# The MLP of a two-block transformer step as two Strassen passes with the hidden layer in DRAM

## The reference

```
h2 = rms_norm(x, norm2_g)
u = jnp.square(jax.nn.relu(jnp.einsum('bsd,df->bsf', h2, w_up)))      # 1024 x 1024 times 1024 x 4096
x = x + jnp.einsum('bsf,fd->bsd', u, w_down)                          # 1024 x 4096 times 4096 x 1024
```

## Time and profile before

| | |
|---|---|
| median of 3 runs | 2311.85 us (2310.8 to 2312.58) |
| the profiled execution's own time | 2313.34 us |
| its span, first to last instruction | 2311.6 us |
| PE busy | 2233.6 us, 97% |
| DVE, POOL, ACT busy | 1319.2, 941.1 and 802.0 us |
| the MLP block | from 1643.4 us to the end |

### The profile page before, as it was taken

The page is one execution under the profiler, slowest core; times in us unless marked ns, Lnnn a source line. Parts: engine busy times, 40 slices in busy tenths (PEclk is TensorE's granted clock), DMA queues, the critical chain, the costliest instruction groups (busy, mean ns, idle before and its releaser), DMA issues. The chain is left out here.

```text
span 2311.6 us, 30049 instructions
## 1 busy us (share of the span) xinstructions
PE 2233.6 (97%) x10722; PEld 1854.4 (80%) x10722; DVE 1319.2 (57%) x2544; ACT 802.0 (35%) x1491; POOL 941.1 (41%) x732
## 2 busy tenths in 40 slices
PE   7999989999999999999999999999999999999997
PEld 7778777778877888888888788888888888888886
DVE  6666674516444666666666582334365565556467
ACT  5444424200004555555554131212333323323322
POOL 3232445535542322313313364553356355554534
PEclk9999999999999999999999999999999999999999
DMA  6220114212324323323322472222110110110211
GB/s 216 94 75 19 42 55 162 83 65 89 111 97 132 107 79 92 100 66 104 87 82 83 164 254 92 92 100 92 55 55 28 64 63 18 64 64 22 68 46 73
DMA packets 177605, 199.79 MB, mean 86 GB/s; under 512 B 56360, under 2 KB 126536, under 8 KB 177520
## 3 DMA queue, kind: packets, MB, share of 16 engines
q1 hardware_dynamic: 100352, 122.47, 16.1%
q10 hardware_dynamic: 77168, 76.19, 10.6%
HBM read 156.63 MB, written 50.40 MB: 90 GB/s over the span
## 5 line engine op out<-in xcount | busy, mean ns | idle before, releaser
L157 POOL TENSOR_TENSOR w_hi<-w_raw,zero 128x512 fp32r<-128x512 f32 x224 | 271.3, 1241 | 967.3 <-PE ps L202 847.5
L202 PE MATMUL ps<-a_hi,w_hi 128*128 128x512 f32 x1664 | 606.7, 405 | 7.4 <-PEq L1654 3.3
L202 PE MATMUL ps<-a_hi,w_lo 128*128 128x512 f32 x1664 | 586.8, 393 | 0.0
L202 PE MATMUL ps<-a_lo,w_hi 128*128 128x512 f32 x1664 | 584.7, 392 | 0.0
L202 PEld LDWEIGHTS ps<-a_hi,w_lo 128*128 128x128 f32 x1664 | 313.8, 189 | 69.3
L202 PEld LDWEIGHTS ps<-a_hi,w_hi 128*128 128x128 f32 x1664 | 314.8, 189 | 62.5 <-issue 9.2
L202 PEld LDWEIGHTS ps<-a_lo,w_hi 128*128 128x128 f32 x1664 | 315.2, 189 | 53.4
L2342 DVE TENSOR_TENSOR res<-res,ps 128x512 f32<-128x512 f32 x384 | 244.7, 682 | 118.0 <-PE ps L202 108.6
L162 POOL TENSOR_TENSOR w_lo<-w_raw,w_hi 128x512 fp32r<-128x512 f32 x224 | 299.7, 1370 | 4.4
L202 PE MATMUL ps<-w_hi,a_hi 128*128 128x512 f32 (+1 forms) x640 | 245.7, 384 | 7.5 <-PEq L1123 2.2
L202 PE MATMUL ps<-w_hi,a_lo 128*128 128x512 f32 (+1 forms) x640 | 244.1, 381 | 0.0
(11 more groups left out here) (206 smaller groups left out, 3301.9 us busy)
## 6 DMA issues: line engine op xcount, KB each, us to landing
w_raw<-in_w_in_dram SPq DMA_DIRECT2D x32, 1024.0 KB, 5.2
feat_fm<-stage ACTq DMA_DIRECT2D x68, 256.0 KB, 2.1
mlp_raw_x<-in_w_up_dram SPq DMA_DIRECT2D x28, 512.0 KB, 4.1
conv_in<-feat_fm ACTq DMA_DIRECT2D x24, 512.0 KB, 5.8
qkv_tm<-stage_tm ACTq DMA_DIRECT2D x5, 2048.0 KB, 6.9
res<-in_x_dram SPq DMA_DIRECT2D x16, 512.0 KB, 6.4
w_raw<-in_w_out_dram SPq DMA_DIRECT2D x8, 1024.0 KB, 5.0
qk_raw<-qkv_tm ACTq DMA_DIRECT2D x32, 256.0 KB, 3.9
```

Of the source, the lines that this page charges most:

```text
L157: hi = nc.gpsimd.tensor_tensor(w_hi[slot][:, k:k + 2, :], w_raw[:, k:k + 2, :], zero[:, 0:1].unsqueeze(2).to_broadcast([P, 2, CW]), ALU.add)
L202: last = nc.tensor.matmul(out_of(o), lhs, rhs(o), start=first and n == 0, stop=final and n == 2)
```

## The change

The MLP becomes two passes with the hidden layer u in DRAM between them. The norm n3 gets a function of its own (`phase_norm_last`) and also prepares operand sums for the first pass.

1. **Up pass, Strassen** over tokens, model features and hidden features: eight groups of 512 hidden features, seven products of 24 matmuls each (`up_tile`). ACT copies the first product of each quarter of u from PSUM to `mlp_acc` (`copy`), DVE adds the others (`add`, 128x1024). A finished quarter is taken by one DVE instruction, `scalar_tensor_tensor` with max 0 and mult, which gives relu squared in place, and ACT's queue stores it to `u_fm` in DRAM (`finish`). The operand sums of the activations are made once, in the norm; the sums of the weights are made by DVE (`up_sum`).
2. **Down pass, Strassen** with groups of 1024 hidden features: four groups of seven steps, each one product of 4 token tiles, 4 k-tiles and 3 passes, 48 matmuls. The quarters of u are loaded back from DRAM (`load_part`), summed by DVE (`staged_sum`), copied by ACT (`staged_high`) and subtracted by DVE (`staged_low`); a quarter of w_down is loaded, summed by POOL (`down_total`), copied by ACT (`down_high`) and subtracted by POOL. x is stored to DRAM in the norm (`x2`) and loaded back into `res`, because `res` serves as scratch in between.
3. The seven down products are ordered m5, m3, m2, m1, m6, m4, m7.

The core of the diff:

```diff
+            DOWN = ("m5", "m3", "m2", "m1", "m6", "m4", "m7")
...
+                            if p == "m6":
+                                sp.wait_ge(w_ready, NU + s + 1)
+                                load_down(g, 1, 0)
...
+                    for s in range(ND):                      # POOL
+                        g, p = s // 7, DOWN[s % 7]
+                        if p == "m3":
+                            pool.wait_ge(b_in, 16 * GROUPS + 32 * g + 16)
+                            pool.wait_ge(c_in, 16 * (g + 1))
+                            down_total(r0, r0, r1, ALU.subtract)
+                        if p == "m1":
+                            pool.wait_ge(a_in, 16 * GROUPS + 16 * (g + 1))
+                            down_total(r1, r1, r2, ALU.add)
+                        if p == "m6":
+                            pool.wait_ge(combined, down_sum(s) - 1)
+                            down_total(r0, r0, r1, ALU.add)
+                        if p == "m4":
+                            pool.wait_ge(b_in, 16 * GROUPS + 32 * g + 32)
+                            down_total(r0, r0, r2, ALU.subtract)
+                        if p == "m7":
+                            pool.wait_ge(combined, down_sum(s) - 1)
+                            down_total(r0, r0, r1, ALU.add)
+                        pool.wait_ge(w_high, NU + s + 1)
+                        for k in range(4):
+                            ins = nc.gpsimd.tensor_tensor(down_slot(w_lo, s)[:, k, :], raw_of[p][:, k, :],
+                                                          down_slot(w_hi, s)[:, k, :].bitcast(F32), ALU.subtract)
+                        ins.then_inc(w_ready, 1)
...
+                    for s in range(ND):                      # PE
+                        pe.wait_ge(w_ready, NU + s + 1)
+                        pe.wait_ge(u_lo, SPLIT_UP + 4 * s + 4)
...
+                        for t in range(4):
+                            if s < 2:
+                                pe.wait_ge(ev_p, 8 * GROUPS - 1 + s)
+                            else:
+                                pe.wait_ge(ev_p, 8 * GROUPS + 4 * (s - 2) + t + 1)
...
+                    for s in range(ND):                      # ACT
+                        if s + 1 < ND:
+                            act.wait_ge(mm_p, NU + 4 * s)
+                            down_high(s + 1)
+                        if s + 2 < ND:
+                            staged_high(s + 2)
...
+                        if (c, n + 1) in DONE:               # DVE, end of add(i, n) of the up pass
+                            dve.wait_ge(ev_p, i * 8 + (n + 1))
+                            nc.vector.scalar_tensor_tensor(acc[:, c, :], acc[:, c, :], 0.0, acc[:, c, :],
+                                                           ALU.max, ALU.mult).then_inc(u_done, 1)
...
+                    for s in range(ND):                      # DVE
+                        if s + 2 < ND:
+                            staged_sum(s + 2)
+                        if s < 2:
+                            dve.wait_ge(*n_stored.at(16 * (s + 1)))
+                        for t in range(4):
+                            down_add(s, t)
+                            if s + 2 < ND and t < 2:
+                                staged_low(s + 2, (2 * t, 2 * t + 1))
...
+                    for t in range(4, NT):                   # POOL, end of phase_norm_last
+                        pool.wait_ge(n_hi.sem, hi0 + t + 1)
+                        toks = slice((t - 4) * P, (t - 3) * P)
+                        nc.gpsimd.tensor_tensor(raw_c[:, :, toks], turned_row(t - 4, 0), turned_row(t, 4), ALU.add).then_inc(p_sum, 1)
+                        nc.gpsimd.tensor_tensor(turned_row(t - 4, 4), turned_row(t - 4, 4), turned_row(t, 4), ALU.add).then_inc(p_sum, 1)
+                        pool.wait_ge(u_sum, t + 1)
+                        nc.gpsimd.tensor_tensor(turned_row(t, 0), turned_row(t, 0), turned_row(t - 4, 0), ALU.add).then_inc(p_sum, 1)
```

More of the change, by code:

```diff
@@ L2147, in combine, with body, down_total @@
+                    def body(i, first, last):
+                        for p in UP[2 if first else 0:]:
+                            up_low(i, p, last)
+                    periods(pool, body)
+                    def down_total(dst, a, b, op):
+                        for k in range(4):
                             last = nc.gpsimd.tensor_tensor(dst[:, k, :], a[:, k, :], b[:, k, :], op)
                         last.then_inc(combined, 1)
[L2150 to L2156 removed]
@@ L2202, in product, with up @@
-                    def product(i, p, count, before):
-                        high, low, o = quarter(w_hi, p), quarter(w_lo, p), int(p[1]) - 1
-                        pe.wait_ge(w_ready, count)
-                        pe.wait_ge(u_lo, i * 14 + (OPERANDS.index((p, 1)) + 1))
+                    def up(i, p, last):
+                        pe.wait_ge(w_ready, i * 7 + (UP.index(p) + 1))
+                        for fb in range(2):
+                            mm = up_tile(p, fb, last)
+                        mm.then_inc(mm_p, 1)
@@ L2239, in _ @@
-                    for q in range(2):
-                        pe.wait_ge(ev_fm, u0 + q + 1)
-                        fm_half(start, q, q, 1).then_inc(mm_fm, 1)
-                    periods(pe, body)
+                            for k in range(4):
+                                mm = three_passes(lambda _: ps[:, 4 * (s % 2) + t, :], high[:, k, toks], low[:, k, toks],
+                                                  lambda _: wh[:, k, :], lambda _: wl[:, k, :], (0,), k == 0, k == 3)
+                            mm.then_inc(mm_p, 1)
@@ L2264, in body, with staged_high @@
+                    def staged_high(s):
+                        if s >= 2 and PARTS[DOWN[s % 7]][1] is None:
+                            act.wait_ge(*staged_in(s))
+                        for k in range(4):
+                            if PARTS[DOWN[s % 7]][1] is not None:
+                                act.wait_ge(u_sum, NT + summed[s] + k + 1)
+                            nc.scalar.activation(down_operand(a_hi, s)[:, k, :], total(s)[:, k, :], ACT.Copy).then_inc(u_hi, 1)
                     def body(i, first, last):
-                        def multiplied(p):
-                            return i * 28 + (tiles(p) + 4)
```

796 lines of the change are left out of this document (549 added, 247 removed).

## The result

The changed kernel takes 2339.23 us (median of 4 runs, 2338.08 to 2340.06) where the kernel before takes 2311.8 (4 runs on the same chip, 2310.8 to 2312.58): 1.0119 times as long, with a 95% interval of 1.0101 to 1.0136. It is slower by 27 us, as forecast in sign and cause (2328.0, range 2296 to 2348), by 11 us more than the forecast had it.

The account below looks back on a forecast made before the run. PE was taken to bound the kernel before, POOL's chain the new down pass. Up matmuls 304.7, turn 0.9, crossing 9.9, down pass 377.4, tail 3.6 make 696.5 against 680.3: 16.2 us more, 2328.0 us, range 2296 to 2348.

Parts of the forecast that it names:

- The mechanism: Down pass: PE waits for POOL's chain of 12.4 us a step against PE's 10.9, lengthened by turns with DVE.
- rarely met: Rival, down pass: POOL's chain seldom meets DVE; with no meetings, period 84.0 and 2285 us; chance 0.17.
- PE stays the bound: Rival, down pass: POOL's work, 61 of 76 us a group, keeps ahead of PE; 2256 us; chance 0.04.
- DVE becomes the bound: Rival, down pass: DVE's list sets the period, 103 us halfway to all meetings; 2361 us; chance 0.13.
- The period: Down group: 84.0 us undisturbed plus 24 meetings at 0.44, 10.6 us, makes 94.7 us.
- The lower clock: Clock drop behind the long gap before m4 in the down pass: 0 to 3.4 us, taken as 0.
- the first starts ... with less work around it: Down pass ends: four periods less 1.4 us for lighter work at start and end, 377.4 us.
- The crossing: Norm to MLP: 1 us delay, 5.5 us PE idle behind POOL's last additions, 3.4 us clock; 9.9 together.
- with more meetings 13: Norm to MLP: upper case of the 9.9 us cost, 13 us if DVE and POOL meet more often.
- The up pass: Up pass: PE never waits, 38.1 us a group, and all 43.5 us of saved matmuls are kept.
- What lies around the span: Time outside the profiled span, 2313.34 less 2311.6 us, was claimed to stay the same.
- the rule of the Trainium skill: Down pass: a DVE and POOL pair excludes each other fully, 1.87 us a pair; period 98.4, time 2343 us.

Follow-up runs that it names:

- e1: The change with DVE's down-pass sums of u and their low parts cut to 8 of 512 columns, result incomplete; 2292.0 us.
- e2: The change with POOL's sums of w_down quarters cut to 8 columns, result incomplete; 2270.5 us.
- e5: e3 plus POOL making the w_down sum of the next step ahead of the current step's low part, with a buffer for m7's sum; 2302.9 us.
- e6: e3 plus DVE instead of POOL making the w_down sums from the third step on, two steps ahead; 2285.1 us.
- e10: The change with the edits of e6 and e8, m5's weight low part made inside the norm, and POOL's last-tile token sums behind the barrier; 2280.1 us.
- e8: The change with relu squared made by Relu and Square on ACT instead of one DVE instruction; 2335.2 us.
- e11: e10 with the weight sum of m7 moved back from DVE to POOL; 2289.6 us.
- e3: The change with the w_down quarter for m4 and m7 in its own buffer and loaded a group early; 2320.0 us.
- e4: The change with DVE's relu squared cut to 8 of 1024 columns, result incomplete; 2332.9 us.

## Why the prediction was right, and where it was off

- **The mechanism** held: PE is paced in the down pass by POOL's chain of sum, copy, subtraction and one load, and that chain is lengthened by turns with DVE. e1 removes the turns (84.9 against a forecast of 84.0 without them) and e2 the sums from the chain (78.2, and 77.4 in a steady group, against PE's 76.3). The rivals "rarely met" and "PE stays the bound" are refuted by these two. "DVE becomes the bound" did not happen in the change, but is the next limit: it is what e5, e6 and e10 ran into.
- **The period**: 95.7 against 94.7. The chain from the end of m5 on PE (2060.2) to the start of m7 (2133.94) lasts 73.7 us, against 62.2 + 10.6 = 72.8 forecast: 26 meetings where I counted 24, and 26 of POOL's 36 instructions in that stretch do last over 1.5 us. Over the whole group POOL's 76.0 less 60.7 makes 35 of 48 at 0.44, and the count of long ones is 33. For DVE the count is 32, while 89.0 less 58.6 makes 27 at 1.11: a met instruction of DVE lost 0.95 us on average, and 1.11 was too high. The gaps stand at four steps and not at two, since each met sum puts the next step later; the sum is the same, because PE's waits all end on one chain. Three periods: 2.9 us of the miss.
- **The lower clock** behind the gaps of a steady group was put at nothing. PE's 81.3 us of busy time in a group are 5 more than 76.3, and the period is that of the chain even so: the chain and not PE sets the next start. That is an argument; no run tried it. Behind a long gap I had read 6.8 us at the lower clock out of a mean of 0.58 over 7 us, and so 3.4 us lost; that mean gives 5.9 and 2.9. Behind the first MLP product its 24 matmuls took 8.30 us where 5.44 is the pitch at full clock, 2.9 us lost.
- **The step that failed** is the start of the down pass ("the first starts ... with less work around it"): I took 1.4 us off the four periods, and there was a gap of 5.45 us before m3 instead. I had followed ACT's wait for the stores into the up pass's groups ("ends about 7 us in"), but not for the last group, where the weight copy of m3 stands behind the last store. I had also costed relu squared at nothing there. With the last group's end, 3.5 us of the miss; e8 gets 2.8 of it back. A gap of 2.94 us before m3 stays there with relu squared on ACT.
- **The crossing**: the first MLP product was forecast for 1631.3 + 48 x 0.2267 + 0.9 + 5.5 = 1648.6, and 1649.6 with the 1 us of delay put in the norm, and came at 1650.41. That delay didn't show: the seventh turn starts at 1630.19 where it was 1630.23 before. But PE stood for 7.11 us and not 5.5. POOL's last token sums took 1.7 us each and not 1.3, in turns with DVE's differences; the prediction had named the meetings but put in none ("with more meetings 13"). 0.8 us of the miss.
- **The up pass**: no wait in seven groups, and one of 1.26 us before m6 of the eighth (POOL's `low`, met by DVE's first `low` for the down pass). From the first MLP product to the first down matmul it is 299.9 us, against 1296 x 0.2267 + 3.4 = 297.2: 2.7 us of the miss. So of the 43.5 us all but about 3 were kept.
- **What lies around the span**: the forecast was worked out on a span of 2311.6 and a median of 2311.85, 0.2 us apart; now span and median are 1.5 apart. 1.3 us. This is no work of the kernel: each profiled execution takes 1.7 to 1.8 us more than its span, and the one before happened to be 1.5 us slower than its median.

Together 2.9 + 3.5 + 0.8 + 2.7 + 1.3 = 11.2 us, the distance from 2328.0 to 2339.2. All of them are on the same side. The first four are places where I had taken too few meetings, or no queue, for want of a row; the last is chance.

By the rule of the Trainium skill (page "SBUF — State Buffer", section "SBUF: two separate sides": whichever of the two starts first keeps the shared port for its whole instruction) the period was put at 98.4 and the time at 2343. The measured 95.7 and 2339 lie between that and the forecast. Experiment 1 shows the rule's kind plainly: a DVE instruction of 8 columns takes 152 ns alone and up to 1278 ns in the same list, about as long as one of POOL's (1.265 us), and ends with it, while POOL's time is unchanged. What the rule to the letter misses is a size: in a sequence a pair takes 1.72 and not 1.87 us.

What stays open: how much of the 2.94 us gap before m3 that e8 leaves is the sum's meetings; what the lower clock costs in the down pass; what makes the 2.1 us of the up pass that neither the gap of 1.26 us nor the clock makes; and e11's places, which were read from its trace, and not tested alone.

## What to carry to other kernels

Saved matmuls are worth their time only while everything that prepares their operands keeps ahead of them; here 43.5 us of matmuls were saved and a net 71 lost around them (27.4 + 43.5), most of them to a chain of sum, copy and subtraction that had no step of slack, and to the turns that lengthened it (e1 gives back 47). Follow such a chain through each engine's list for the first and the last round too, where a store or a barrier stands in it that the steady rounds don't have. And count the instructions of DVE and POOL that both work on SBUF alone together: here moving a sum from a full DVE to POOL made the period longer (e11), moving all sums from POOL to DVE made it shorter (e6), and making the sums a step ahead of their use gained 17 us on e3 (e5). Additions with a PSUM source took no part in the turns.

## What the runs showed of the hardware

- A DVE instruction with two SBUF sources that meets one of POOL can be held until the end of POOL's, whatever its own size: with 8 columns it takes 152 ns alone and up to 1278 ns (e1, L2748), with 512 columns 675 alone and 1756 in the middle. What a meeting can cost, 1.13 and 1.1 us, doesn't shrink with its size. Whether fewer and larger instructions would lose less was not tried.
- A meeting costs POOL 0.44 us in most cases (1.74 us where it takes 1.27 alone), but more where DVE has several in a row: 10.65 us for four, one of them 3.64, in e11.
- Relu squared as one scalar_tensor_tensor over two SBUF sources of 128x1024 takes 1224 ns at its least, the same as the tensor_tensor of that size with a PSUM source in the earlier trace rows (1218), and less than twice the 675 ns of a tensor_tensor of half the size with two SBUF sources. Its two sources are the same tile; with two different ones the least is 1285. The Trainium skill, page "Vector Engine (DVE) Microarchitecture Reference", section "7. Points that are easy to get wrong", says that this instruction with two sources in SBUF that are not bfloat16 runs at half the throughput; measured against those tensor_tensor rows, this trace does not bear it out.
- The down matmuls, twelve behind one wait, ran at 0.2267 us: 48 of them from 2049.34 to 2060.22 make a step of 10.88 us. The 0.2333 of the earlier trace rows was thus no price of these matmuls' shape, which is the same.
- Behind a short gap of PE the clock fell in some places and not in others, and the length of the gap alone doesn't tell: behind 2.40 us it stayed at full speed (change, 2180.16, a mean of 1.00 over the next 3.5 us), behind 1.79 us it was mostly at the lower level (e4, 2092.61, a mean of 0.56).
